# A two-block transformer kernel on one core: the hand-over from the convolution's input product to its output product is re-ordered

## The chip, the cores and the metric

The kernel runs on one core of one Trainium2 chip. The time is the device time of one execution in microseconds (us). The core has TensorE (PE: matmuls; its weight loads are listed as PEld), VectorE (DVE), ScalarE (ACT), GpSimd (POOL) and SyncE (SP, which issues the loads).

## The reference, cut to what matters

Batch 1, 256 tokens, width 2048, float32. The first block is the one that the change touches:

```python
cond = silu(c)
sh1, sc1, g1, sh2, sc2, g2 = split(cond @ mod_w + mod_b, 6)       # "modulation", mod_w is 2048 x 12288
h = rms_norm(x, norm1_g) * (1 + sc1) + sh1
a, gt = split(h @ conv_w_in + conv_b_in, 2)                       # conv-in, 2048 x 4096
u = a * sigmoid(gt)                                               # the gated units
u = depthwise_causal_conv(u, conv_dw_w, 31 taps) + conv_dw_b
u = silu(layer_norm(u, conv_ln_g, conv_ln_b))                     # over the 2048 channels
x = x + (1 + g1) * (u @ conv_w_out + conv_b_out)                  # conv-out, 2048 x 2048
h = rms_norm(x, norm2_g) * (1 + sc2) + sh2
x = x + (1 + g2) * (relu(h @ mlp_w1)**2 @ mlp_w2)
```

A second block (attention, gated feed-forward, final norm) follows. It is not touched.

## The kernel before

**One stream of loads.** All weights come in one ordered list, `stream`, in tiles of 512 KB, issued by SP in that order. A load goes into a slot and waits until the tile that was in the slot has been read. Up to `n_first` items there are 12 slots; behind it there are 6 (`slot_of`, `earlier_in_slot`), because slots 6 to 11 (`stage2`) lie in the same memory as `whi` and `wlo`, the split copies of conv-out's weights. `consume()` handles the next item of the stream: it emits the instructions that read it. Kinds: "n" is a conv-in tile (multiplied in plain float32), "w" a tile that ACT rounds into `whi` and DVE (or POOL) subtracts into `wlo` for three-pass matmuls (ring of three, `NPAIR`), "m" a tile of modulation weights.

**Modulation.** A group of 16 "m" tiles gives 1024 modulation columns. There are three ways to sum it: on DVE (a multiply, then 15 multiply-adds in a buffer of `accs`), "aside" (ACT multiplies, POOL adds; three product buffers), or on PE (`mod_on_pe`: two one-row matmuls a tile, accumulated in two banks). `mod_end` turns the sum into columns by 8 small matmuls and `mod_columns` (three small DVE instructions). Block 0 has 80 aside tiles (`mods`): 66 (`N_MOD_IN`) go with conv-in, 4 (`N_MOD_TAIL`) into the tail, 10 in among conv-out's tiles 3 to 13. The fourth quarter of norm 2 is summed on PE, all 16 tiles in the tail.

**Emission.** The program is one Python pass; each engine executes its own queue strictly in the order of emission. While products are emitted, `between_tiles()` runs after each PE tile: up to two `tasks`, up to two `delayed` tasks whose tile has come (`later(n, task)`), one of `slow`, up to `TAPS_A_TILE` steps of `dve_taps`, one of `pe_taps`. `run_one()` takes the first of `tasks`, or if none is left the first of `delayed`, due or not.

**The convolution.** Conv-in is 8 chunks p = 0..7 of 8 tiles; chunk p gives the gated units `U` of channel tiles 2p and 2p+1. Its epilogue: ACT evacuates two banks; one tile later `gated` emits 8 transposes (PE), two sigmoids (ACT) and two DVE instructions that write `U`. The taps of 14 channel tiles run on DVE (`DVE_JOBS`; a step is two 128x256 multiply-adds; job (11, 12) and job (13,) become ready with chunk 6, job (15,) with chunk 7), those of tiles 3 and 14 on PE (`pe_job`, 31 matmuls with diagonal matrices, in parts of 8). When channel tiles 0 to 12 are done, `ln_provisional` sums them on PE and DVE makes the provisional mean `m0`; 7 `centre` steps subtract it (DVE), their squares go through ACT and PE (`ln_square`). Tiles 13, 14, 15 follow in `ln_late`. Then `layer_norm()` and its `finish` tasks make `hhi`/`hlo`, conv-out's left side.

**The tail** is the code in `build_program` behind `products(0, n1)`: the rest of the tasks, then a loop with two tasks, one part of `pe_taps`, up to four steps of taps, one of `slow` and one `consume()` a turn. Then all tail tiles are consumed, and, ahead of `layer_norm()`,

```python
while len(pair_ready) < 2:
    consume()
```

which puts the splits of conv-out's first two weight tiles in front of the layer norm in every queue.

## Time and profile before

| | |
|---|---|
| time, median of 3 runs | 2690.1 us (2689.15 to 2693.38) |
| the profiled execution's own time | 2690.38 us |
| its span in the trace | 2688.1 us |
| TensorE busy | 2541.3 us (95%) |
| VectorE, ScalarE, GpSimd busy | 1755.5, 1146.5, 373.6 us |
| conv-in's last part, tail, conv-out (windows) | 141.6 to 332.7, to 424.6, to 531.5 us |
| HBM read | 640.60 MB |

The span runs from the first to the last instruction. A busy share is an average over all stages; the tail is where TensorE's share falls most in this part. In the timeline each row is a run of like instructions of one engine: start, length, what it does, how many, and in brackets how long the engine had been idle and what ended that.

### The profile page before, as it was taken

The page shows a single profiled execution, that of the slowest core. Times are in us where ns is not written, and L with a number is a line of the kernel's source. Part 1 is how long each engine was busy: PE and PEld are TensorE (multiplying, and loading weights), DVE is VectorE, ACT ScalarE, POOL GpSimd, SP SyncE. Part 2 cuts the span into 40 slices and gives each one's busy share as a digit, 9 for nine tenths or more (in the row PEclk, how much of TensorE's full clock was granted, in tenths as well). Part 3 has the DMA queues.
Part 4 walks back from the last instruction along what each step waited for, and adds up shares of the span by engine and source line. Part 5 has one row for each costly group of instructions (what it writes and reads, how often), then busy time and mean ns, then how long its engine had stood idle before and what let it go on. Part 6 is the DMA issues. An engine that isn't in the chain of part 4 may idle for free.

```text
span 2688.1 us, 29379 instructions
## 1 busy us (share of the span) xinstructions
PE 2541.3 (95%) x10784; PEld 1977.6 (74%) x10784; DVE 1755.5 (65%) x2124; ACT 1146.5 (43%) x1441; POOL 373.6 (14%) x177
## 2 busy tenths in 40 slices
PE   4899977989999999999899999999899999999998
PEld 2354444778888888888678788788688888888886
DVE  5678847677877867768665455786577654555455
ACT  2144426444344344344445454544444434443443
POOL 1048823112222222222000000000000000000000
PEclk9999988989999999999899999999899999999999
DMA  8989736668888888888754647886488766666664
GB/s 299 375 294 386 250 120 220 209 210 297 301 301 283 308 289 302 305 293 291 195 169 129 180 134 222 304 273 225 157 282 275 241 189 194 188 189 194 190 188 141
DMA packets 340158, 644.66 MB, mean 240 GB/s; under 512 B 30000, under 2 KB 63440, under 8 KB 338992
## 3 DMA queue, kind: packets, MB, share of 16 engines
q1 hardware_dynamic: 338752, 642.09, 73.1%
q8 instruction: 87, 1.43, 0.2%
q0 software_dynamic: 448, 0.43, 0.1%
q14 instruction: 55, 0.45, 0.1%
q10 hardware_dynamic: 816, 0.26, 0.0%
HBM read 640.60 MB, written 2.10 MB: 239 GB/s over the span
## 4 chain that ended last, share of the span: by engine, by line
PE 83%; DVE 8%; DMA 4%; ACT 2%; POOL 2%; issue 1%; SPq 0%; DVEq 0%; ACTq 0%; POOLq 0%
PE bank L84 83%; DVE bank L84 3%; DMA stage<-in_mod_w 2%; DVE wlo L84 1%; POOL R L84 1%; DVE acc L84 1%; DVE scr L84 1%; ACT whi L84 1%; ACT scr L84 1%; DVE X L84 1%; DVE R2f L84 0%; DVE R L84 0%; DMA stage<-in_w_in 0%; SPq L84 0%; DMA stage<-in_mlp_w 0%
## 5 line engine op out<-in xcount | busy, mean ns | idle before, releaser
L84 DVE TENSOR_TENSOR wlo<-stage,whi 128x1024 fp32r<-128x1024 f32 x688 | 868.4, 1264 | 673.7 <-ACT whi L84 653.8
L84 ACT ACTIVATE whi<-stage 128x1024 fp32r<-128x1024 f32 x752 | 795.8, 1059 | 1022.3 <-PE bank L84 921.7
L84 PE MATMUL bank<-whi,hhi 128*128 128x512 f32 x2016 | 806.5, 400 | 31.6 <-DVE hlo L84 18.9
L84 PE MATMUL bank<-wlo,hhi 128*128 128x512 f32 x2016 | 791.6, 393 | 0.0
L84 PE MATMUL bank<-whi,hlo 128*128 128x512 f32 x2016 | 791.3, 393 | 0.0
L84 PEld LDWEIGHTS bank<-whi,hhi 128*128 128x128 f32 x2016 | 383.2, 190 | 119.2 <-ACT scr L84 23.5
L84 PEld LDWEIGHTS bank<-wlo,hhi 128*128 128x128 f32 x2016 | 383.3, 190 | 81.0 <-issue 3.1
L84 PEld LDWEIGHTS bank<-whi,hlo 128*128 128x128 f32 x2016 | 382.7, 190 | 81.4
L84 PE MATMUL bank<-whi,uhi 128*128 128x512 f32 x992 | 390.0, 393 | 0.8 <-POOL wlo L84 0.8
L84 PE MATMUL bank<-whi,ulo 128*128 128x512 f32 x992 | 389.8, 393 | 0.0
L84 PE MATMUL bank<-wlo,uhi 128*128 128x512 f32 x992 | 387.0, 390 | 0.0
L84 POOL TENSOR_TENSOR wlo<-stage,whi 128x1024 fp32r<-128x1024 f32 x64 | 166.0, 2594 | 632.1 <-ACT whi L84 620.7
L84 PE MATMUL bank<-stage,hx 128*128 128x512 f32 x512 | 234.0, 615 | 10.1 <-DMA stage<-in_conv_w_in 5.8
L84 DVE SCALAR_TENSOR_TENSOR acc<-stage,CS,acc 128x1024 f32<-128x1024 f32 x165 | 213.1, 1292 | 17.1 <-DMA stage<-in_mod_w 15.0
L84 POOL TENSOR_TENSOR R<-R 128x1024 f32<-128x1024 f32 x75 | 183.1, 2443 | 270.6 <-ACT R L84 262.8
L84 PEld LDWEIGHTS bank<-wlo,uhi 128*128 128x128 f32 x992 | 186.3, 188 | 41.8 <-issue 0.2
L84 PEld LDWEIGHTS bank<-whi,uhi 128*128 128x128 f32 x992 | 186.4, 188 | 40.9 <-issue 2.2
L84 PEld LDWEIGHTS bank<-whi,ulo 128*128 128x128 f32 x992 | 186.3, 188 | 40.7
L84 PEld LDWEIGHTS bank<-stage,hx 128*128 128x128 f32 x512 | 99.4, 197 | 134.8 <-issue 120.9
L84 DVE SCALAR_TENSOR_TENSOR bank<-R2f,DW,bank 128x256 f32<-128x256 f32 x418 | 165.4, 483 | 0.0
L84 DVE SCALAR_TENSOR_TENSOR R<-stage,CS,R 128x1024 f32<-128x1024 f32 x105 | 134.3, 1279 | 13.9 <-DMA stage<-in_mod_w 11.6
L84 PE MATMUL bank<-ident,scr 128*128 128x128 f32 x524 | 81.3, 299 | 38.2 <-DVE scr L84 33.3
(120 smaller groups left out, 1182.9 us busy)
## 6 DMA issues: line engine op xcount, KB each, us to landing
stage<-in_mlp_w SPq DMA_DIRECT2D x256, 512.0 KB, 5.4
stage<-in_mod_w SPq DMA_DIRECT2D x192, 512.0 KB, 7.6
stage<-in_w_ada SPq DMA_DIRECT2D x192, 512.0 KB, 5.2
stage<-in_w_in SPq DMA_DIRECT2D x136, 512.0 KB, 3.9
stage<-in_w_ffn_gate SPq DMA_DIRECT2D x88, 512.0 KB, 4.4
stage<-in_w_ffn_up SPq DMA_DIRECT2D x88, 512.0 KB, 4.4
stage<-in_w_ffn_down SPq DMA_DIRECT2D x88, 512.0 KB, 4.2
stage<-in_conv_w_in SPq DMA_DIRECT2D x128, 256.0 KB, 7.7
```

The lines of the kernel that those rows point to most:

```text
L84: made = fn(*args, **kw)
```

## The change

It has five parts.

1. **Slots.** `n_first` grows by the length of the tail, so the tail's tiles use all 12 slots. The two conv-out tiles ahead of `layer_norm()` are no longer consumed there.
2. **Modulation.** The tail holds 8 tiles of the last group (PE) and 9 aside tiles, 17 in place of 20. The group's other 8 tiles go on in a buffer of `accs` on DVE (`mod_goes_on`: one multiply, two adds of the PE row onto one row of the buffer, 7 multiply-adds), among conv-out's tiles 3 to 18 with the 5 aside tiles that are left. Its columns come by the ordinary `mod_end`.
3. **Pace of the taps.** In place of 5 steps a tile, steps are emitted until an estimate of their end passes the estimate of the tile's end by `LEAD` (8, from the ninth tile before the end of conv-in 2); in the tail three steps a turn in place of four.
4. **Gated units.** The epilogue is cut into `turn` (transposes, sigmoids) and `gated` (the DVE part and what follows), emitted 2 and 3 tiles later; for p < 3 one tile later, and for the last chunk at once. `L_SQUARE` is 3.
5. **Tail.** After the tasks, four tiles are consumed at once. Tile 14's 31 tap matmuls are one part; its evacuation (`pe_ends`) is emitted only when no DVE taps are left. The warming square root is left out of conv-in, and a Silu is emitted behind the layer norm's square root.

```diff
-N_MOD_TAIL = 4
-N_MOD_OUT = 14
-TAPS_A_TILE = 5
+N_MOD_TAIL = 9
+N_MOD_PE = 8
+N_MOD_OUT = 18
+LEAD = 8.0
+LEAD_LAST = 2.0
+TILE_US = 4.1
+STEP_US = 0.8
...
-L_SQUARE = 2
+L_SQUARE = 3
+L_TURN = 2
+L_GATED = 3
...
+        pace = {"tile": 0.0, "taps": 0.0, "lead": LEAD}
...
             for _ in range(min(len(slow), 1 + len(slow) // 10)):
...
-            for _ in range(min(len(dve_taps), TAPS_A_TILE)):
+            pace["tile"] += TILE_US
+            if not dve_taps:
+                pace["taps"] = max(pace["taps"], pace["tile"])
+            while dve_taps and pace["taps"] < pace["tile"] + pace["lead"]:
+                pace["taps"] += STEP_US
...
-                if m["aside"] == "PE":
+                if m["aside"] == "PE" and kt < N_MOD_PE:
...
+                elif m["aside"] == "PE":
+                    mod_goes_on(m, kt, w, c, landed)
+                    stage_free[s] = [m["last"]]
                 elif m["aside"]:
...
-                                  start=(kt == 0), stop=(kt == NKT - 1), signal=(j == 1),
+                                  start=(kt == 0), stop=(kt == N_MOD_PE - 1), signal=(j == 1),
...
+        def mod_goes_on(m, kt, w, c, landed):
+            if kt > N_MOD_PE:
+                m["last"] = V.put(nc.vector.scalar_tensor_tensor, out=m["buf"][1], in0=w, scalar=c,
+                                  in1=m["buf"][1], op0=ALU.mult, op1=ALU.add, after=[landed, m["last"]])
+                return
+            run_until(accs.any_free)
+            m["buf"] = accs.take()
+            m["ring"] = accs
+            rows, buf = m["last"], m["buf"][1]
+            t = V.put(nc.vector.tensor_scalar, buf, w, c, None, ALU.mult, after=[landed, m["cond"]] + m["buf"][2])
+            for j in range(2):
+                row = buf[0:1, j * 512:(j + 1) * 512]
+                m["last"] = V.put(nc.vector.tensor_tensor, row, row, groups[m["group"]][j][0:1, :], ALU.add,
+                                  after=[t, rows])
+            group_free[m["group"]] = [m["last"]]
         def mod_columns(m, bank, t):
...
         def mod_end(m):
...
-            if m["aside"] == "PE":
-                row = []
-                for j in range(2):
-                    row.append(tiles.take())
-                    i, buf, free = row[j]
-                    row[j] = (i, buf, A.put(nc.scalar.activation, buf[0:1, :], groups[m["group"]][j][0:1, :], ACT.Copy,
-                                            after=[m["last"]] + free))
-                group_free[m["group"]] = [row[0][2], row[1][2]]
-                def columns():
-                    b, bank, free = misc.take()
-                    for j in range(8):
-                        _, buf, made = row[j // 4]
-                        t = T.put(nc.tensor.matmul, bank[:, j:j + 1], buf[0:1, (j % 4) * 128:(j % 4) * 128 + 128],
-                                  ones[0:1, 0:1], start=True, stop=True, after=[made, consts] + free)
-                    for i, _, _ in row:
-                        tiles.give(i, t)
-                    misc.give(b, mod_columns(m, bank, t))
-                later(2, columns)
-                return
...
+        pe_ends = deque()
...
-                if hi_ == TAPS:
+                def end():
...
-            for lo in range(0, TAPS, 8):
-                pe_taps.append(lambda lo=lo: part(lo, min(lo + 8, TAPS)))
+                if hi_ == TAPS:
+                    if ct == PE_JOBS[0]:
+                        end()
+                    else:
+                        pe_ends.append(end)
+            for lo in range(0, TAPS, 8 if ct == PE_JOBS[0] else TAPS):
+                pe_taps.append(lambda lo=lo: part(lo, min(lo + (8 if ct == PE_JOBS[0] else TAPS), TAPS)))
...
-                    def gated():
-                        two = [misc.take(), misc.take()]
+                    state = {}
+                    def turn():
+                        two = state["two"] = [misc.take(), misc.take()]
...
-                        i, sig, free = tiles.take()
+                        state["values"] = t
+                        state["sig"] = i, sig, free = tiles.take()
...
-                            r = A.put(nc.scalar.activation, sig[:, k * S:(k + 1) * S], two[1][1][:, k * S:(k + 1) * S],
-                                      ACT.Sigmoid, bias=PA[:, 32 + ct:33 + ct], after=[gates_in, params["A"]] + free)
+                            state["sigmoid"] = A.put(nc.scalar.activation, sig[:, k * S:(k + 1) * S],
+                                                     two[1][1][:, k * S:(k + 1) * S], ACT.Sigmoid,
+                                                     bias=PA[:, 32 + ct:33 + ct],
+                                                     after=[gates_in, params["A"]] + free)
+                        misc.give(two[1][0], state["sigmoid"])
+                    def gated():
+                        b, bank, _ = state["two"][0]
+                        i, sig, _ = state["sig"]
...
-                                                in0=two[0][1][:, k * S:(k + 1) * S], scalar=PA[:, 16 + ct:17 + ct],
+                                                in0=bank[:, k * S:(k + 1) * S], scalar=PA[:, 16 + ct:17 + ct],
...
-                                                after=[t, r, params["A"], consts])
-                        misc.give(two[1][0], r)
-                        misc.give(two[0][0], u_ready[ct])
+                                                after=[state["values"], state["sigmoid"], params["A"], consts])
+                        pace["taps"] += STEP_US
+                        misc.give(b, u_ready[ct])
...
-                    later(1, gated)
+                    if p == NKT // 2 - 1:
+                        tasks.append(turn)
+                        tasks.append(gated)
+                    elif p < 3:
+                        later(1, turn)
+                        later(1, gated)
+                    else:
+                        later(L_TURN, turn)
+                        later(L_GATED, gated)
...
+                    pace["taps"] += STEP_US
...
+            A.put(nc.scalar.activation, ST[:, 62:63], eps, ACT.Silu, after=[consts])
...
-        tail = mix(mod_pairs(0, 1, 3, aside="PE", soon=True), mods[N_MOD_IN:N_MOD_IN + N_MOD_TAIL])
-        seq += tail + co[:3] + mix(co[3:N_MOD_OUT], mods[N_MOD_IN + N_MOD_TAIL:]) + co[N_MOD_OUT:]
-        n_tail = n_first[0] + len(tail)
+        last = mod_pairs(0, 1, 3, aside="PE")
+        tail = mix(last[:N_MOD_PE], mods[N_MOD_IN:N_MOD_IN + N_MOD_TAIL])
+        seq += tail + co[:3] + mix(co[3:N_MOD_OUT], mods[N_MOD_IN + N_MOD_TAIL:] + last[N_MOD_PE:]) + co[N_MOD_OUT:]
+        n_tail = n_first[0] = n_first[0] + len(tail)
...
-                if g == hi_ - 6:
+                if g == n1 - 9:
+                    pace["lead"] = LEAD_LAST
+                if g == hi_ - 6 and lo:
...
-        while tasks or delayed:
+        while tasks:
...
-            for _ in range(min(len(dve_taps), 4)):
+        for _ in range(4):
+            consume()
+        while dve_taps or pe_taps or slow or tasks or delayed or pe_ends or len(ln["late"]) < len(LN_LATE):
+            if pe_taps:
+                pe_taps.popleft()()
+            for _ in range(min(len(dve_taps), 3)):
...
-        while dve_taps or pe_taps or slow or tasks or delayed or len(ln["late"]) < len(LN_LATE):
+            if not dve_taps and pe_ends:
+                pe_ends.popleft()()
...
-            if pe_taps:
-                pe_taps.popleft()()
-            for _ in range(min(len(dve_taps), 4)):
-                dve_taps.popleft()()
...
-            consume()
-        while len(pair_ready) < 2:
...
```

## Rows read from the trace of the kernel before

**Rows 1.** The page: its span.
```profile
span 2688.1 us, 29379 instructions
```

**Rows 2.** Windows: PE, PEld, DVE, ACT, POOL busy (count), granted clock, DMA share, GB/s.
```profile
141.60:332.70 191.10, 186.95 (x510) 92.16 (x511) 154.47 (x389) 90.51 (x120) 143.98 (x67) 0.98 0.90 313
332.70:424.60 91.90, 66.56 (x215) 35.42 (x214) 46.79 (x99) 29.88 (x43) 24.18 (x11) 0.84 0.49 162
424.60:531.50 106.90, 98.84 (x416) 79.63 (x416) 76.23 (x69) 59.06 (x75) 29.77 (x10) 0.93 0.64 199
```

**Rows 3.** Timeline of PE: conv-in's end, the tail, conv-out's beginning.
```profile
274.26 0.33 PE L84 MATMUL bank<-ident,scr 128*128 128x128 f32 x1 [3.06 <-ACT scr L84]
...
275.89 22.12 PE L84 MATMUL bank<-stage,hx 128*128 128x512 f32 x48
...
308.67 24.20 PE L84 MATMUL bank<-stage,hx 128*128 128x512 f32 x56
332.71 5.78 PE L84 MATMUL bank<-R2f,ones 128*128 128x256 f32 x26
345.94 3.58 PE L84 MATMUL bank<-ones,R 128*128 128x1 f32 x16 [7.45 <-POOL R L84]
...
392.06 20.76 PE L84 MATMUL bank<-stage,CS 128*1 128x512 f32 x48
...
424.61 0.76 PE L84 MATMUL bank<-whi,hhi 128*128 128x512 f32 x1 [11.79 <-DVE hlo L84]
...
432.22 1.94 PE L84 MATMUL bank<-ones,scr 1*128 1x1 f32 x16
```

**Rows 4.** Timeline of DVE, chunk 6's gated units to conv-out.
```profile
309.67 0.88 DVE L84 SCALAR_TENSOR_TENSOR R2f<-bank,PA,scr 128x256 f32<-128x256 f32 x2 [5.61 <-ACT scr L84]
...
311.36 23.59 DVE L84 SCALAR_TENSOR_TENSOR bank<-R2f,DW,bank 128x256 f32<-128x256 f32 x60
...
338.98 2.21 DVE L84 TENSOR_TENSOR R2f<-R2f,scr 128x512 f32<-128x512 f32 x1
...
353.03 0.87 DVE L84 SCALAR_TENSOR_TENSOR R2f<-bank,PA,scr 128x256 f32<-128x256 f32 x2
...
380.60 0.42 DVE L84 TENSOR_TENSOR R2f<-R2f,scr 128x256 f32<-128x256 f32 x1 [8.07 <-ACT R2f L84]
380.94 0.48 DVE L84 SCALAR_TENSOR_TENSOR bank<-R2f,DW,bank 128x256 f32<-128x256 f32 x1
...
414.38 2.59 DVE L84 TENSOR_TENSOR wlo<-stage,whi 128x1024 fp32r<-128x1024 f32 x2 [30.09 <-ACT whi L84]
...
494.84 1.23 DVE L84 TENSOR_TENSOR wlo<-stage,whi 128x1024 fp32r<-128x1024 f32 x1 [1.49 <-ACT whi L84]
```

**Rows 5.** Timeline of ACT, same stretch.
```profile
304.10 0.66 ACT L84 ACTIVATE R2f<-bank 128x256 f32<-128x256 f32 x2 [10.95 <-DVE bank L84]
...
338.25 1.15 ACT L84 ACTIVATE R<-stage,CS 128x1024 f32<-128x1024 f32 x1 [0.81 <-POOL R L84]
339.30 1.06 ACT L84 ACTIVATE scr<-bank 128x512 f32<-128x512 f32 x2
...
351.25 0.84 ACT L84 ACTIVATE scr<-bank,PA 128x256 f32<-128x256 f32 x2 [9.59 <-PE bank L84]
...
418.26 0.51 ACT L84 ACTIVATE scr<-scr,ST 128x256 f32<-128x256 f32 x1 [1.10 <-DVE scr L84]
```

**Rows 6.** Groups by form in the tail, PE: tile 14's taps.
```profile
L84 PE MATMUL bank<-R2f,hx 128*128 128x256 f32 x62 | 16.1, 417 | 0.0
```

**Rows 7.** Groups by form in conv-out, DVE: count, busy us, mean ns, idle before.
```profile
L84 DVE TENSOR_TENSOR wlo<-stage,whi 128x1024 fp32r<-128x1024 f32 x30 | 53.3, 1799 | 24.3 <-ACT whi L84 22.1 <-issue 2.3
L84 DVE TENSOR_TENSOR scr<-bank,G 128x512 f32<-128x512 f32 x6 | 4.1, 684 | 0.0
```

**Rows 8.** The tile `acc` from 250 to 650 us: duration ns min/median/max.
```profile
L84 DVE SCALAR_TENSOR_TENSOR acc<-stage,CS,acc x15: 1273/1279/3422, 562.1 to 622.8; 128x1024 f32<-128x1024 f32 x15
L84 DVE TENSOR_SCALAR acc<-stage,CS x1: 734/734/734, 535.5 to 535.5; 128x1024 f32<-128x1024 f32 x1
```

## The prediction

> **What bounds the kernel now.** First the windows [rows 2]: up to 332.7 us PE is busy 186.95 of 191.10 us, in the tail 66.56 of 91.90, in conv-out 98.84 of 106.90. DMA moves 162 GB/s in the tail against 313 before it, so the change is about the tail and what it takes from its neighbours. The timelines then say what the tail waits for. PE's last wait ends with DVE's `hlo` [rows 3]. DVE does its last tap at 380.94, its last small work near 384, and then stands 30.09 us until conv-out's first `whi` exists [rows 4]: the two splits stand ahead of the layer norm in its queue, their weights stand behind the modulation tiles in the stream, and PE reads the last twelve of these in 20.76 us, 1.73 each [rows 3]. So the end of the tail is set by stream order, not by the convolution. Before that, DVE waits 8.07 us for tile 14's evacuation with one step of taps unfinished [rows 4]; and chunk 7's units, whose transposes stand behind columns that wait 7.45 us for POOL, reach DVE at 353.03 although conv-in ends at 332.5 [rows 3, 4]. With the stream out of the way, DVE's work and its own waits set the end.
>
> **The change step by step. (a) When chunk 7's units come.** Chunk 6's went to DVE at 309.67 [rows 4]. Their transposes move one PE tile back, 24.20/7 = 3.46 us [rows 3]; against that PE's stall of 3.06 us at 274.26, a wait for an evacuation that ACT could not start, gets a tile of slack and goes, with some 1.5 us of half-rate matmuls behind it (behind it 6 tiles took 22.12 us where 6 x 3.46 = 20.7 were due [rows 3]). That leaves 309 (up to 313 if the stall's time isn't kept). Job (11, 12) takes 309.67 to 334.95, 25.3 us [rows 4], so it ends at 334.3; ACT evacuates it (0.66, as [rows 5], first) and does the sigmoid (0.84 [rows 5]), and DVE the first unit (0.44 [rows 4]): tile 14's `U` is there at 336.3. The other path is POOL: the last conv-in product on ACT stood at 338.25, and the evacuation right behind it [rows 5]. If POOL keeps its time, evacuation, transposes (1.0), sigmoid and unit give 343; part of its backlog came from ACT standing 10.95 us for a tap evacuation [rows 5], and should shrink. I take 338, bounds 335.5 and 343.
>
> **(b) A new stall on DVE.** Counting steps through `between_tiles` with the new pace (4.1 a tile, 0.8 a step, lead 2 from tile 55), 7 steps go out after tile 58, then 5, 5, 5, 6, and 5 after tile 63: the 32nd of job (11, 12), its end, is among the last, with one step of job 13. So `ln_provisional` is still in `delayed` when the tail begins. The loop's first turn emits, in this order: all 31 tap matmuls of tile 14 (PE), three steps of job 13 (DVE, 2.4 us), the columns of the aside group (PE, then three small DVE instructions), the sums of tiles 0 to 12 (PE), `m0` (DVE). PE's queue is in order: taps 16.1 us [rows 6], columns 3.58, sums 5.78 [rows 3], `m0` 0.43. `m0` ends at 338 + 0.4 + 16.1 + 3.6 + 5.8 + 0.4 = 364.3, and DVE, which reaches it near 341.5, has stood over 20 us. Before, the sums ran right behind conv-in and the taps came in four parts with squares between. This is what the part of 31 costs; its gain is that nothing of it waits later. Everything behind on DVE (taps, centring) waits with it; ACT's squares too. The columns' wait for POOL (345.94 before [rows 3]) hides under the taps.
>
> **(c) From `m0` to the layer norm's root.** DVE has left 23 taps of tile 13 and 31 of tile 15, at 23.59/60 = 0.393 and a little more for first ones: 21.7 us. Seven centrings lie between 0.68 alone (the same size in [rows 7]) and 2.21 beside POOL [rows 4]; nine aside tiles now run there, not four, so I take 7.3 in all (bounds 4.6 and 15). Tile 13's end and centring: 1.3. Last tap at 394.6. Tile 14's evacuation no longer stops a tap (8.07 us saved, but it now follows): copy, add, centring, square of 15, then the same of 14, about 4.9 us to the end of the root, from the spacing of those steps before. Root at 399.5.
>
> **(d) To the first matmul of conv-out.** Before, from the root's end (418.77 [rows 5]) to 424.61: 5.84, with one split in it. Now three splits (1.22 each, of which two come extra, the slots holding the weights already) stand before the first `finish`: 5.84 + 2.44 = 8.3. Start at 407.8, against 424.61: **16.8 us gained**. Loads can't take it back: twelve slots let the 17 tiles and conv-out's first ones be issued turns ahead, and SP waited for consumption.
>
> **(e) Tail tiles.** PE sheds 8 x 1.73 = 13.8 us, but in (b) it isn't this that DVE waits for, so I book nothing. If it were needed behind `m0`, PE has 8 squares and 7 tiles, some 21 us, under DVE's 30.
>
> **(f) Conv-out, 106.90 us before.** The columns of the last group are now 16 full-height records, 3.58 in place of 1.94 [rows 3]: +1.6. The bank pair of the half group is now freed by DVE's two row adds at k = 8, which conv-out's second chunk needs: DVE does split, multiply (0.734 [rows 8]) and two adds, each under 0.684 (full height, same width [rows 7]), after a split that itself waits for PE: +2 (bounds 0 and 6). DVE gets 0.73 + 7 x 1.28 + 1.3 = 11.0 us of new work [rows 7, 8]. Against it, splits cost 1.799 us on average [rows 7] where undisturbed ones cost 1.23 [rows 4], 17 us of 53.3, and five of ten aside tiles leave conv-out: about 8.5 back. Conv-out's later tiles come every 1.23 + 1.49 = 2.72 us and leave DVE idle for the 1.49 [rows 4], which holds a 1.28 multiply-add. Three more loads stand in the mixed stretch. For these together +0.5 (bounds -5 and +16). Sum **+4.1**.
>
> **(g)** The table loads left out of conv-in (ACT) and the Silu load lie beside other work: nothing, at most 1.3 us each.
>
> **Sum.** The profiled execution took 2690.38, its span 2688.1 [rows 1]; 2690.4 - 16.8 + 4.1 = 2677.7. The runs' median is 0.3 lower: **2677.5**.
>
> **Rivals.** *No stall at `m0`*: if the sums get ahead of tile 14's taps (my count of steps is one off only at the last tile, and one more turn would not do it, but an early `run_one` would), DVE runs through from 338.9: `m0` 0.4, 60 taps 24.1, centring and tile 13's end 8.3, root at 376.6, first matmul at 384.9, 23 us sooner: 2654.6. For it speaks that 30.09 and 8.07 us of waits are there to be had [rows 4]; against it the order of emission. Chance 0.14.
>
> *DVE becomes conv-out's bound* (the other side): new work 11.0 us not hidden at all, and half contended. [Rows 8] show a multiply-add of 3.42 us beside one of POOL's subtractions, 2.14 over the median; 7 x 2.14/2 = 7.5. With +1.6 and +2, conv-out is 22.1 longer, and the time is 2690.4 - 16.8 + 22.1 = 2695.7, 2695.4 at the median. It decides once more than 16.8 us of conv-out's additions show. Against it: POOL's adds end before most of these multiply-adds are due. Chance 0.10. The Trainium skill, GPSIMD Engine Reference, section Specifications, says that GpSimd's SBUF interfaces are shared with VectorE and contend when a VectorE instruction has two SBUF inputs, which this multiply-add has and the taps (PSUM accumulator) have not; it speaks against moving tiles to DVE while POOL adds. The trace agrees where both run [rows 7, 8]; by the rule with every one of the seven contended the time would be 7.5 us more again, 2702.9.
>
> *PE's tail stays at half rate.* The tap matmuls of tile 14 started at the lower of TensorE's two clocks after PE had idled; the granted clock of the tail is 0.84 [rows 2]. A 512-wide record at the upper clock takes 20.76/48 = 0.43 us [rows 3], so a 256-wide one at the lower takes as much; 62 of them are 26.8 in place of 16.1 us: `m0` 10.7 later, 2688.2. Chance 0.08; all 62 took 16.1 before.
>
> **How the numbers follow.** My forecast has 0.60, the rivals 0.14, 0.10, 0.08, and 0.08 is for what I haven't seen. The likeliest case's own range: (a) -2.5 to +5, (c) -3 to +8, (f) -7 to +8, not all at one end: 2668 to 2688. To hold 8 in 10 it reaches down to the no-stall case and up to the clock case: **2655 to 2689**. A measurement tells about 0.2% (5.4 us) from no change. Faster by more (below 2684.7): most of the forecast, 0.52, the first rival 0.14, and 0.07 of the rest: 0.73. Within: 0.14. Slower: 0.13.
>
> **What the profile would show.** (a) DVE writes chunk 7's units at 336 to 343, with ACT's tap evacuation just before the sigmoid. (b) PE shows 62 records of `R2f,hx` in one row, then the columns, then 26 of `R2f,ones`; DVE stands about 17 us before `MC` and again before the small `scr<-bank`, 20 to 24 in all. If these waits are missing, the first rival holds. (c) Last tap near 395, no 8 us wait in front of it. (d) The 30.09 us wait is gone, and three `wlo` stand between the reciprocal and the first `hlo`. (f) conv-out lasts 107 to 115 us; a wait of PE for DVE's `acc` or `R` at the second chunk; splits near 1.23 us once POOL is quiet. Wrong I would be through a wait on a load in the tail, through POOL's nine aside tiles holding ACT (which every square and evacuation passes), or through conv-out running longer than 123 us.

## The result and the profile after

The changed kernel takes 2695.7 us (median of 20 runs) against 2689.8 of the kernel before in the same rounds (20 runs): ratio 1.0021, 95% interval 1.0014 to 1.0028. It is slower by 6 us. The prediction said 2677.5, faster, with a range of 2655 to 2689. The profiled execution took 2699.4, its span is 2697.1. Of all runs in this document one, of *units early*, fell in a slower state of the chip (3212 us at a granted clock of 0.76) and is not counted. In what follows L90 is the same recording helper as L84 before.

The windows of the kernel after, over the same three stretches as [rows 2]:

```profile
141.60:332.70 191.10, 181.27 (x489) 90.14 (x489) 142.20 (x357) 83.81 (x113) 133.38 (x63) 0.97 0.86 301
332.70:424.60 91.90, 64.40 (x204) 34.36 (x203) 62.55 (x129) 36.56 (x49) 46.53 (x20) 0.85 0.48 160
424.60:531.50 106.90, 90.39 (x379) 73.59 (x380) 74.29 (x77) 51.62 (x68) 14.53 (x5) 0.89 0.63 205
```

All three stretches hold less of PE's work than before. The first is a surprise: it lies ahead of the tail, I had costed nothing in it, and it lost 5.7 us of PE and 12.3 of DVE. PE's timeline after, with the time that it stood and the releaser at the end of a row:

```profile
172.51 1.94 PE L90 MATMUL bank<-ident,scr 128*128 128x128 f32 x8 [3.51 <-DVE R2f L90]
...
251.05 0.33 PE L90 MATMUL bank<-ident,scr 128*128 128x128 f32 x1 [1.65 <-ACT scr L90]
...
284.16 0.33 PE L90 MATMUL bank<-ident,scr 128*128 128x128 f32 x1 [2.11 <-ACT scr L90]
...
318.51 0.33 PE L90 MATMUL bank<-ident,scr 128*128 128x128 f32 x1 [2.00 <-ACT scr L90]
...
339.57 2.74 PE L90 MATMUL bank<-stage,hx 128*128 128x512 f32 x6
351.08 2.24 PE L90 MATMUL bank<-ident,scr 128*128 128x128 f32 x8 [8.77 <-ACT scr L90]
...
356.56 13.65 PE L90 MATMUL bank<-R2f,hx 128*128 128x256 f32 x62
370.05 1.84 PE L90 MATMUL bank<-ones,R 128*128 128x1 f32 x16
371.76 5.86 PE L90 MATMUL bank<-R2f,ones 128*128 128x256 f32 x26
...
412.68 4.39 PE L90 MATMUL bank<-stage,CS 128*1 128x512 f32 x8
425.39 0.76 PE L90 MATMUL bank<-whi,hhi 128*128 128x512 f32 x1 [8.32 <-ACT scr L90]
...
466.98 0.77 PE L90 MATMUL bank<-whi,hhi 128*128 128x512 f32 x1 [8.29 <-DVE acc L90]
```

Where [rows 3] had one wait of 3.06 us on its way to the tail (and the same timeline one of 0.77), there are four now, 9.3 us in all, with half-rate matmuls behind them (eight transposes in 1.94 us at 172.51, in 1.04 at 169.16 before), and conv-in's last products end at 342.3 in place of 332.7 or so. Chunk 7's transposes then wait 8.77 us more for ACT. The 62 tap records, the columns and the sums come in the order that step (b) said. Conv-out's first matmul starts at 425.39, which is 0.8 *later* than before, and in conv-out there is a new wait of 8.29 for the row adds. DVE's timeline after:

```profile
156.61 14.98 DVE L90 SCALAR_TENSOR_TENSOR bank<-R2f,DW,bank 128x256 f32<-128x256 f32 x38
171.49 0.88 DVE L90 SCALAR_TENSOR_TENSOR R2f<-bank,PA,scr 128x256 f32<-128x256 f32 x2
...
321.85 0.88 DVE L90 SCALAR_TENSOR_TENSOR R2f<-bank,PA,scr 128x256 f32<-128x256 f32 x2 [6.64 <-ACT scr L90]
...
353.45 0.88 DVE L90 SCALAR_TENSOR_TENSOR R2f<-bank,PA,scr 128x256 f32<-128x256 f32 x2 [5.49 <-ACT scr L90]
354.24 2.44 DVE L90 SCALAR_TENSOR_TENSOR bank<-R2f,DW,bank 128x256 f32<-128x256 f32 x6
371.93 0.23 DVE L90 TENSOR_TENSOR MC<-bank,PB 128x4 f32<-128x4 f32 x2 [15.25 <-PE bank L90]
...
377.65 0.43 DVE L90 TENSOR_SCALAR scr<-bank 128x256 f32<-128x256 f32 x1 [5.29 <-PE bank L90]
...
449.47 12.74 DVE L90 TENSOR_TENSOR wlo<-stage,whi 128x1024 fp32r<-128x1024 f32 x4 [0.56 <-issue]
462.13 0.68 DVE L90 TENSOR_TENSOR scr<-bank,G 128x512 f32<-128x512 f32 x1
...
464.77 0.75 DVE L90 TENSOR_SCALAR acc<-stage,CS 128x1024 f32<-128x1024 f32 x1
465.56 1.27 DVE L90 TENSOR_TENSOR acc<-acc,bank 1x512 f32<-1x512 f32 x2
```

The 30.09 us wait of [rows 4] is gone. In its place DVE stands 15.25 + 5.29 us at the start of the tail, and everything starts later. The first two rows show where the conv-in part goes wrong. In the kernel before 18 taps stand between the units of chunks 0 and 1, and PE's transposes find the bank free:

```profile
156.93 7.14 DVE L84 SCALAR_TENSOR_TENSOR bank<-R2f,DW,bank 128x256 f32<-128x256 f32 x18
163.98 0.87 DVE L84 SCALAR_TENSOR_TENSOR R2f<-bank,PA,scr 128x256 f32<-128x256 f32 x2
```

Now 38 do, because the pace lets the taps run 8 us ahead: fifteen steps go out at once. The other end of it is on ACT, whose tap evacuations stand in its queue until DVE's last tap, with POOL's products behind them. ACT after:

```profile
247.78 0.66 ACT L90 ACTIVATE R2f<-bank 128x256 f32<-128x256 f32 x2 [13.16 <-DVE bank L90]
...
281.93 0.66 ACT L90 ACTIVATE R2f<-bank 128x256 f32<-128x256 f32 x2 [11.43 <-DVE bank L90]
...
315.24 0.66 ACT L90 ACTIVATE R2f<-bank 128x256 f32<-128x256 f32 x2 [12.33 <-DVE bank L90]
...
349.40 1.15 ACT L90 ACTIVATE R<-stage,CS 128x1024 f32<-128x1024 f32 x1 [1.34 <-POOL R L90]
```

Of these the first was 3.85 before, the second 11.32, the third 10.95 [rows 5]. ACT's last product of conv-in comes at 349.40 where it came at 338.25 [rows 5], and chunk 7's evacuation stands right behind it.

### The profile page after: what moved, and what is told of

It reads as the page before. It is cut to its first block, busy times and chain, and to the rows that moved or that the text cites. A ratio compares the mean times of both kernels' runs of the same rounds, so it can differ in the third digit from the quotient of the medians.

```text
span 2697.1 us, 29330 instructions
## 1 busy us (share of the span) xinstructions
PE 2534.3 (94%) x10752; PEld 1976.7 (73%) x10752; DVE 1763.1 (65%) x2134; ACT 1142.9 (42%) x1437; POOL 369.7 (14%) x177
## 4 chain that ended last, share of the span: by engine, by line
PE 83%; DVE 8%; POOL 3%; DMA 3%; ACT 2%; issue 1%; SPq 0%; DVEq 0%; ACTq 0%; POOLq 0%
PE bank L90 83%; DVE bank L90 3%; POOL R L90 3%; DMA stage<-in_mod_w 2%; DVE wlo L90 1%; DVE scr L90 1%; DVE R2f L90 1%; ACT scr L90 1%; ACT whi L90 1%; DVE acc L90 1%; DVE X L90 0%; ACT hhi L90 0%; DMA stage<-in_w_in 0%; DMA stage<-in_conv_w_out 0%; ACT R L90 0%
## 5 line engine op out<-in xcount | busy, mean ns | idle before, releaser
L90 DVE TENSOR_TENSOR wlo<-stage,whi 128x1024 fp32r<-128x1024 f32 x688 | 859.8, 1251 | 648.4 <-ACT whi L90 634.5
L90 ACT ACTIVATE whi<-stage 128x1024 fp32r<-128x1024 f32 x752 | 795.5, 1059 | 1036.8 <-PE bank L90 928.0
L90 PE MATMUL bank<-whi,hhi 128*128 128x512 f32 x2016 | 806.1, 400 | 39.3 <-ACT scr L90 8.3
L90 PE MATMUL bank<-whi,hlo 128*128 128x512 f32 x2016 | 791.3, 393 | 0.0
L90 PE MATMUL bank<-wlo,hhi 128*128 128x512 f32 x2016 | 791.1, 392 | 0.0
L90 PEld LDWEIGHTS bank<-whi,hhi 128*128 128x128 f32 x2016 | 382.9, 190 | 126.2 <-ACT scr L90 17.1
L90 PEld LDWEIGHTS bank<-wlo,hhi 128*128 128x128 f32 x2016 | 383.1, 190 | 80.9 <-issue 3.1
L90 PEld LDWEIGHTS bank<-whi,hlo 128*128 128x128 f32 x2016 | 382.3, 190 | 81.5
L90 PE MATMUL bank<-whi,ulo 128*128 128x512 f32 x992 | 389.7, 393 | 0.0
L90 PE MATMUL bank<-whi,uhi 128*128 128x512 f32 x992 | 389.7, 393 | 0.0
L90 PE MATMUL bank<-wlo,uhi 128*128 128x512 f32 x992 | 387.1, 390 | 0.0
L90 POOL TENSOR_TENSOR wlo<-stage,whi 128x1024 fp32r<-128x1024 f32 x64 | 165.5, 2585 | 658.0 <-ACT whi L90 650.7
L90 PE MATMUL bank<-stage,hx 128*128 128x512 f32 x512 | 235.0, 617 | 7.4 <-DVE hx L90 4.2
L90 DVE SCALAR_TENSOR_TENSOR acc<-stage,CS,acc 128x1024 f32<-128x1024 f32 x172 | 220.0, 1279 | 15.6 <-DMA stage<-in_mod_w 13.5
L90 PEld LDWEIGHTS bank<-wlo,uhi 128*128 128x128 f32 x992 | 186.3, 188 | 41.8 <-issue 0.2
L90 PEld LDWEIGHTS bank<-whi,ulo 128*128 128x128 f32 x992 | 186.3, 188 | 40.6
L90 PEld LDWEIGHTS bank<-whi,uhi 128*128 128x128 f32 x992 | 186.4, 188 | 39.6 <-issue 0.5
L90 POOL TENSOR_TENSOR R<-R 128x1024 f32<-128x1024 f32 x75 | 179.6, 2397 | 255.7 <-ACT R L90 247.7
L90 PEld LDWEIGHTS bank<-stage,hx 128*128 128x128 f32 x512 | 100.3, 199 | 131.5 <-issue 121.8
L90 DVE SCALAR_TENSOR_TENSOR bank<-R2f,DW,bank 128x256 f32<-128x256 f32 x418 | 165.2, 482 | 0.0
L90 DVE SCALAR_TENSOR_TENSOR R<-stage,CS,R 128x1024 f32<-128x1024 f32 x105 | 136.4, 1299 | 12.7 <-DMA stage<-in_mod_w 10.2
L90 PE MATMUL bank<-ident,scr 128*128 128x128 f32 x524 | 83.0, 301 | 52.2 <-DVE scr L90 33.3
```

The lines of the kernel that those rows point to most:

```text
L90: made = fn(*args, **kw)
```

## The experiments

Each was timed in five rounds beside the kernel before, whose medians lay between 2688.5 and 2690.8. Differences between two rows below are differences of their medians, and good to about 2 us for that reason. "Conv-out starts" is the first matmul with `whi`.

| run | us | ratio to before, 95% interval | conv-out starts |
|---|---|---|---|
| changed kernel | 2695.7 | 1.0014 to 1.0028 | 425.4 |
| units early | 2691.3 | 0.9993 to 1.0012 | 421.2 |
| fixed pace | 2681.4 | 0.9959 to 0.9981 | 411.6 |
| lead 2 | 2679.5 | 0.9951 to 0.9975 | 408.5 |
| pace and units | 2676.5 | 0.9935 to 0.9965 | 407.5 |
| row first | 2688.4 | 0.9984 to 1.0005 | 424.2 |
| parts of 8 | 2685.0 | 0.9975 to 0.9996 | 415.7 |
| pace, units, row | 2668.3 | 0.9910 to 0.9937 | 406.1 |
| all four edits | 2658.2 | 0.9871 to 0.9896 | 395.3 |
| all four, six slots | 2661.5 | 0.9884 to 0.9911 | 398.8 |
| all four, 12 tiles on PE | 2654.0 | 0.9857 to 0.9882 | 397.3 |
| all four, 15 on PE | 2662.3 | 0.9880 to 0.9907 | 406.3 |
| the same, six slots | 2668.3 | 0.9897 to 0.9928 | 412.4 |
| before, no splits ahead of the norm | 2688.2 | 0.9986 to 1.0003 | 424.7 |
| the same, twelve slots | 2686.9 | 0.9980 to 0.9998 | 421.8 |

**Units early.**

```
-L_TURN = 2
-L_GATED = 3
+L_TURN = 1
+L_GATED = 1
```

> The changed kernel with the transposes, sigmoids and gated units emitted one tile behind their chunk, as before the change. Theory A (units that come late hold ScalarE in front of tap evacuations, and so GpSimd's sums and TensorE's transposes): GpSimd's last sum before the tail's ends some 4 to 8 us earlier than its 361.6 us, and since the tap job of tiles 11 and 12 is then emitted before conv-in ends, the provisional sums stand ahead of tile 14's taps and VectorE's stall of 15 + 5 us before m0 shrinks to a few us; time about 2680 us. Theory B (GpSimd's own rate of 2.5 us an add sets chunk 7's units, whatever the order): GpSimd's last sum stays within 2 us of 361.6, chunk 7's units at 353; only the stall changes, time 2685 to 2690.

2691.3. Theory A gave 2680 and is wrong for this edit by itself; theory B's 2685 to 2690 doesn't hold either. The waits for tap evacuations stay (13.47, 15.41 and 13.63 us on ACT), PE stands 3.50 us at 170.75 as in the changed kernel, and chunk 7's units come at 359.45, 6.0 *later* than there. What is gained lies behind them: `m0` now stands ahead of tile 14's taps (DVE starts it at 349.62, for 377.65), though 15.62 us of wait in front of `MC` stay.

**Fixed pace.**

```
-            while dve_taps and pace["taps"] < pace["tile"] + pace["lead"]:
-                pace["taps"] += STEP_US
+            for _ in range(min(len(dve_taps), 5)):
                 dve_taps.popleft()()
```

> The changed kernel with five steps of taps a tile again, in place of the paced emission; units stay late. Theory A: the wait of TensorE for VectorE at 172 us (3.5 us) goes, since 15 steps no longer stand ahead of chunk 1's units; the waits of ScalarE for a tap evacuation (13.2, 11.4, 12.3 us) shrink by one to two tiles' time each where they are not fed by the loop; conv-in ends 4 to 8 us earlier; the stall before m0 stays; time about 2689 us. Theory B: conv-in's last units at 353, time 2694 to 2697.

2681.4, 14.3 us less than the changed kernel, and well below the 2689 of theory A. ACT's longest wait for a tap evacuation is 8.37 us, as in the kernel before; PE stands only 1.37 us in conv-in and 5.23 in front of chunk 7's transposes, and chunk 7's units come at 335.70; the stall on DVE stays (13.42 in front of `MC`). That the pace costs is shown; whether through its lead or its clock the run on the lead tells.

**Pace and units.** The two edits above together.

> Both: units one tile behind their chunk and five steps of taps a tile, so conv-in is emitted as before the change, with the change's tail, slots and modulation behind it. Theory A: conv-in as before (last product near 332.5, GpSimd's last sum near 346), chunk 7's units near 343 since nothing stands before them, no stall of 20 us before m0, first conv-out matmul near 400; with conv-out's added 7.6 us the time is about 2674 us. Theory B: the tail's end moves by the stall alone, first matmul 405 to 410, time 2680 to 2685. If the tail's own parts were the loss, the time stays near 2695.

2676.5, conv-out at 407.5: between what the two theories gave. Chunk 6's units come as before the change (309.70), chunk 7's 8.0 us sooner than there (345.03), and `m0` gets ahead of tile 14's taps (DVE does it at 339.99), which is the "no stall" rival's condition. Yet 13.07 us of wait in front of `MC` stay, since the columns are still emitted behind the 31 taps. So the rival was half right: there are two things behind the taps, and either holds DVE.

**Row first.** The half group's ninth tile, whose row adds free the bank pair, moves ahead of the other modulation tiles.

```
-... mix(co[3:N_MOD_OUT], mods[N_MOD_IN + N_MOD_TAIL:] + last[N_MOD_PE:]) ...
+... mix(co[3:N_MOD_OUT], last[N_MOD_PE:N_MOD_PE + 1] + mods[N_MOD_IN + N_MOD_TAIL:]
+                         + last[N_MOD_PE + 1:]) ...
```

> The changed kernel with the ninth tile of the half-and-half modulation group (the one whose row adds free the pair of banks) first among the tiles mixed into conv-out, in place of sixth. Theory: TensorE's wait of 8.3 us for VectorE's row adds at 467 us, and some 2 us at the lower clock behind it, go; VectorE has the same work earlier, where it is the bound, so 1 to 3 us come back; time 2687 to 2690. Rival: the splits of conv-out's weights, held up by GpSimd and by loads, would have made TensorE wait there anyway; the wait then changes its releaser and the time stays within 2 us of 2695.7.

2688.4, 7.3 us less, with conv-in and tail as in the changed kernel. PE's timeline in conv-out has no wait for `acc` left:

```profile
446.45 0.76 PE L90 MATMUL bank<-whi,hhi 128*128 128x512 f32 x1 [5.88 <-DVE wlo L90]
...
465.70 0.47 PE L90 MATMUL bank<-whi,hhi 128*128 128x512 f32 x1 [2.27 <-DVE wlo L90]
```

**Parts of 8.** Tile 14's taps in four parts, as before.

```
-            for lo in range(0, TAPS, 8 if ct == PE_JOBS[0] else TAPS):
+            for lo in range(0, TAPS, 8):
```

> The changed kernel with tile 14's 31 taps given out in four parts (8, 8, 8, 7) as before the change; nothing else. Theory A (the stall on DVE is one of order in PE's queue: the columns and the sums stand behind 62 records of taps): the wait in front of MC falls from 15.25 to about 4 us, m0 comes some 10 us sooner (368 in place of 378), and conv-out's first matmul near 415 in place of 425.4; the conv-in part stays as in the changed kernel. Time 2684 to 2688. Theory B (what sets the end of the tail is something else, the load stream, POOL or ACT's evacuations, and DVE's standing lies beside it): the wait shrinks but conv-out begins at 423 to 425 all the same; 2693 to 2697.

2685.0, 10.7 us less, by this edit alone. Theory A's time and its `m0` (367.93) hold, and the wait in front of `MC` is 5.45. DVE:

```profile
362.21 0.23 DVE L90 TENSOR_TENSOR MC<-bank,PB 128x4 f32<-128x4 f32 x2 [5.45 <-PE bank L90]
...
367.93 0.43 DVE L90 TENSOR_SCALAR scr<-bank 128x256 f32<-128x256 f32 x1 [5.29 <-PE bank L90]
```

**Lead 2.**

```
-LEAD = 8.0
+LEAD = 2.0
```

> The changed kernel with one number edited: the taps are given out at most 2 us ahead of the tiles' clock from the start, in place of 8; so nearly as five a tile, with the units still late. Theory A (what costs in conv-in is the lead: the taps given out ahead stand in DVE's queue before the next chunk's units, and one chunk's 30 us of taps come in a burst before it): ACT's waits for tap evacuations fall from 11 to 13 us to under 9, PE's waits for them go but for one, conv-out begins near 411; 2680 to 2685. Theory B (the lead does nothing; counting by a clock of 4.1 us a tile, with the two extra entries for the units, is what falls out of step with the tiles): 2692 to 2697.

2679.5, 16.2 us less than the changed kernel by one number: theory A, just below its bounds. Counting by a pace costs nothing that shows (the fixed pace gave 2681.4); the lead does. PE's waits in conv-in, then chunk 7's units and `m0` on DVE:

```profile
275.11 1.09 PE L90 MATMUL bank<-ident,scr 128*128 128x128 f32 x8 [0.39 <-ACT R2f L90]
...
294.80 1.98 PE L90 MATMUL bank<-R,ones 128*128 128x512 f32 x4 [1.42 <-POOL R L90]
...
333.79 2.24 PE L90 MATMUL bank<-ident,scr 128*128 128x128 f32 x8 [5.23 <-ACT scr L90]
```

```profile
336.15 0.88 DVE L90 SCALAR_TENSOR_TENSOR R2f<-bank,PA,scr 128x256 f32<-128x256 f32 x2 [0.69 <-ACT scr L90]
...
360.75 0.42 DVE L90 TENSOR_SCALAR scr<-bank 128x256 f32<-128x256 f32 x1 [5.30 <-PE bank L90]
```

**Pace, units and row together.**

> The changed kernel with three edits: five steps of taps a tile in place of the paced bursts, the gated units one tile after their chunk as before, and the half group's ninth tile first among conv-out's modulation tiles. Theory A (the costs are separate and add): the pace and the units gave 2676.5 together, the row 7.3 alone; so 2669 (2667 to 2672), with PE's wait for acc (7.68 us there) gone. Theory B (with conv-out beginning 17 us earlier its splits collide with POOL's sums, so the row adds are late whatever their order): 2674 to 2677.

2668.3, 8.2 less than without the row. The costs are separate.

**All four.** Beside these, parts of 8, and the tail's loop takes them up behind the delayed tasks:

```
+            for _ in range(2):
+                if tasks or delayed:
+                    run_one()
             if pe_taps:
                 pe_taps.popleft()()
             ...
-            for _ in range(2):
-                if tasks or delayed:
-                    run_one()
```

> As the run before it (pace, units, row), and tile 14's taps in parts of 8 that stand behind the delayed tasks in the tail's loop, so that the columns of the aside group come ahead of them. Theory A (what is left of the stall, 13.07 us in front of MC with pace and units mended, lies on the path to conv-out): 8 to 12 us less than the run before, 2657 to 2661, conv-out's first matmul at 396 to 399. Theory B (the stall is cover for POOL's sums, for tile 14's evacuation or for conv-out's weights, one of which is late next): 0 to 4 us less, 2665 to 2669, with a new wait of 8 us or more in front of the last taps, the centring or the first whi.

2658.2, 10.1 less again, in theory A's range. DVE waits 2.41 us in front of `MC`, and PE has the columns first:

```profile
342.72 2.23 PE L90 MATMUL bank<-ones,R 128*128 128x1 f32 x16 [2.84 <-POOL R L90]
...
346.65 5.77 PE L90 MATMUL bank<-R2f,hx 128*128 128x256 f32 x16
...
379.02 5.31 PE L90 MATMUL bank<-stage,CS 128*1 128x512 f32 x12
395.26 0.76 PE L90 MATMUL bank<-whi,hhi 128*128 128x512 f32 x1 [10.92 <-ACT scr L90]
```

The next four runs ask which part of the change takes away the 30.09 us wait of before.

**Before, without splits ahead of the norm.**

```
-        while len(pair_ready) < 2:
-            consume()
```

> The kernel before with one part of the change alone: the loop that splits two tiles of conv-out ahead of the layer norm is left out, so that the norm's small work no longer stands behind the splits in DVE's and ACT's queues. Theory A, my prediction's reading of the 30.09 us wait (the splits are in the norm's way, and the norm was ready long before): the norm ends some 25 us sooner, conv-out begins as soon as its first weights have come, at 416 to 418 in place of 424.6; 2682 to 2684. Theory B (the weights of conv-out land late, and the three splits and the first finish then cost as much behind the norm as ahead of it): conv-out begins within 2 us of 424.6; 2688 to 2691.

2688.2 with an interval that holds 1, conv-out at 424.65: theory B. DVE now stands 22.03 us for ACT's square root, which stands in ACT's queue behind products that wait for their tiles (9.57, 8.79 and 5.58 us for loads). The splits were not what held the norm.

**The same with twelve slots.**

```
-        n_tail = n_first[0] + len(tail)
+        n_tail = n_first[0] = n_first[0] + len(tail)
```

> The kernel before with two parts of the change alone: twelve slots through the tail, and no splits ahead of the layer norm; order of taps, pace, units and the half group as before. Theory A (these two take the stream out of the tail's end, and the rest of the change is what gives it back): DVE's 22 to 30 us of waiting at the norm goes, the norm's root ends near 392, conv-out begins at 400 to 408 in place of 424.6; 2666 to 2675. Theory B (the sixteen tiles on TensorE still come too late for it, being read in order at 1.73 us each behind tile 14's taps): conv-out begins at 415 or later, 2680 to 2689.

2686.9, conv-out at 421.82: theory B. The root now ends at 406.3, yet little is won by it. PE reads the last twelve tiles just as before, and the first `whi` starts as it ends. PE, then ACT:

```profile
393.13 20.76 PE L84 MATMUL bank<-stage,CS 128*1 128x512 f32 x48
421.82 0.77 PE L84 MATMUL bank<-whi,hhi 128*128 128x512 f32 x1 [7.92 <-DVE hlo L84]
```

```profile
403.19 1.15 ACT L84 ACTIVATE R<-stage,CS 128x1024 f32<-128x1024 f32 x1 [8.73 <-DMA stage<-in_mod_w]
...
413.98 2.95 ACT L84 ACTIVATE whi<-stage 128x1024 fp32r<-128x1024 f32 x3 [7.72 <-issue]
```

The profile names no releaser for the 7.72 us, but the code does: the buffers of `whi` share memory with the second six slots, so the first `whi` has to wait until PE has read the last modulation tile in them (413.89).

**All four, six slots.** The line above undone.

> The run with all four edits (pace, units, row, parts behind the columns; 2658.2), but the twelve load slots end with conv-in, as before the change: six through the tail and conv-out. Theory A (the tail's end was set by the stream before the change, and the slots are what takes it away; this was what my prediction's gain rested on): the loads are late again, ACT and PE wait for modulation tiles, conv-out begins at 408 to 418 in place of 395.3, 2672 to 2680. Theory B (the order written in the tail is enough, and the loads come in time from six slots too): conv-out begins within 3 us of 395.3, 2657 to 2661.

2661.5: 3.3 us more than with twelve, conv-out 3.6 us later, just outside theory B's bounds. With eight tiles on PE the slots are worth about 3 us; the two intervals overlap a little.

**All four, twelve tiles on PE.** `N_MOD_PE = 12` in place of 8.

> The run with all four edits, with twelve of the half group's sixteen tiles on TensorE in the tail in place of eight, so four multiply-adds fewer on DVE in conv-out and four loads more in the tail. Theory A (with twelve slots the tail has room for them, as my step that booked nothing for PE's share says, and conv-out's start is set by DVE's taps): conv-out begins within 3 us of 395.3, its mixed stretch is 3 to 6 us shorter, 2653 to 2657. Theory B (the stream is the next limit of the tail: a tile of 0.5 MB takes 1.7 us at the 301 GB/s of conv-in): conv-out begins 7 us later and 3 to 6 come back, 2659 to 2663.

2654.0, the fastest version, 34 us under the 2688.5 of the kernel before beside it. Conv-out starts 2.0 later and the rest is shorter by more: theory A.

**All four, fifteen tiles on PE**, and **the same with six slots**.

> The run with all four edits, but fifteen of the half group's sixteen tiles on TensorE in the tail (one left for DVE): the twelve slots with the modulation of before. Theory A (PE's own reading of the tiles, 1.73 us each behind the squares, sets the tail's end, as the 48 records of 20.76 us that end at 413.9 in the run with slots alone say): from twelve to fifteen tiles conv-out begins 5 to 10 us later than the 397.3 of twelve tiles, 2658 to 2664. Theory B (PE has room under DVE's taps, and it was the order of emission alone that held the tail): conv-out begins within 3 us of 397.3; 2651 to 2656.

> As the run before it, with six load slots in the tail. Theory A (slots and PE's share act on one limit: with all the tiles in the tail the stream is late again, and the slots are worth much more than the 3.3 us that they were worth with eight): 8 us or more over the run before it, 2666 or more, with ACT or PE waiting for modulation tiles. Theory B (the slots are worth the same 2 to 4 us here): 2 to 4 us over it.

2662.3, and conv-out starts at 406.3, 9.0 later than with twelve tiles: theory A of the first. PE reads its tiles until 395.0; only then does SP issue conv-out's first load (395.01, after 11.7 us without one), and `whi` waits 6.11 us for it. With six slots it is 2668.3, 6.0 us more: between what the two theories gave, with the waits for modulation tiles that theory A named (four on ACT, 1.57 to 3.90 us, and one of 1.78 on PE). So the slots are worth somewhat more when more tiles pass, but not 8 us. PE and ACT with fifteen and twelve slots:

```profile
381.09 13.89 PE L90 MATMUL bank<-stage,CS 128*1 128x512 f32 x32
406.30 0.77 PE L90 MATMUL bank<-whi,hhi 128*128 128x512 f32 x1 [11.32 <-ACT scr L90]
```

```profile
399.14 1.06 ACT L90 ACTIVATE whi<-stage 128x1024 fp32r<-128x1024 f32 x1 [6.11 <-DMA stage<-in_conv_w_out]
```

## Why the prediction was wrong

Against the 2677.7 of the sum the profiled execution took 2699.4, 21.7 more. Conv-out started 17.6 late (425.4 for 407.8) and took 3.4 more (PE ends it near 539.8: 114.4 for 106.9 + 4.1); the remaining 0.7 lies behind it.

**(a) When chunk 7's units come: the step that failed.** I took 338 with bounds 335.5 and 343; they came at 353.45, 15.4 late, most of the whole error. I worked from 309.67 for chunk 6's, "up to 313", which took conv-in's rhythm as untouched, and counted the new pace only at its end, for the order in (b). But the lead acts from the first chunk: chunk 6's units came at 321.85. The same rule that put fifteen steps at once into DVE's queue was in the diff, and the two prices stood in the rows: 0.393 us a tap, so 20 taps more before chunk 1's units are 7.9 us; and an ACT evacuation that stands 10.95 us [rows 5], with POOL's products behind it. I used the second as a reserve ("should shrink"); it grew, 36.9 us in three waits where it was 26.1, and the last product came 11.2 later. Most of it is there early: chunk 2's units come at 180.89 for 172.59, 8.3 late, chunk 6's 12.2. How it divides between the burst and ACT's waits no run separates. With lead 2 both go (chunk 1's units at 165.59, ACT's three waits 4.86, 2.49 and 4.95), so the lead makes both. Cut to 2 it gives 16.2 us back, the fixed pace 14.3, and chunk 7's units come inside my bounds, at 336.15 and 335.70. With lead 2 the rest follows nearly as summed: `m0` ends at 361.2 for 364.3, conv-out starts at 408.5 for 407.8, the time is 2679.5 for 2677.5. The later units do bring chunk 7's sooner, as I said: 335.70 for 345.03, both with the fixed pace. Yet they cost some 4 to 5 us of the time (2695.7 to 2691.3 alone; 2681.4 to 2676.5 on top of the pace), because with them `m0` stands behind tile 14's taps: that is the stall in (b), and I had not put it down to them.

**(b) The stall.** Right in mechanism, order and size: 15.25 and 5.29 us, 20.5 in all, where I said 20 to 24; 62 records in one row; from the units to `m0`'s end 24.6 us for 26.3. What it costs the kernel: 10.7 us when only the parts are given back, 10.1 on top of the others, with the loop's new order.

**(c) and (d)** held to 2.4 and 1.4 us: from `m0` to the root 37.6 for 35.2, root to matmul 9.7 for 8.3. Two of the centrings beside POOL took 2.40 us, against 0.68 alone.

**(e) PE's tail tiles at nothing: wrong in what it says of before.** In the sum it did no harm, as I had put the whole gain under (d). But the reading that "the end of the tail is set by stream order", cured by slots, is refuted: slots without splits ahead of the norm gain 2.8 us of conv-out's start in the kernel before, and about 3.3 us of the time in the version with all four edits. What holds the tail of the kernel before is PE's reading, in order, behind the last squares, at 1.73 us a tile: with all else mended 15, 12 and 8 tiles on PE start conv-out at 406.3, 397.3 and 395.3. The last step is 2.0 for four tiles, 6.9 us of reading, so at eight the reading sets the start no more. From fifteen to twelve is 8.3 us of the time by the medians (6.7 by the ratios to the kernel before, 0.9894 and 0.9869); below twelve DVE's share in conv-out costs more than the tail gains (2658.2 with eight for 2654.0). In [rows 3] this limit was to be seen: 48 records without a gap end at 412.8, and ACT's first `whi` starts at 413.2.

**(f) Conv-out.** I had +4.1, it was +7.5. The row adds were the mis-sized term: 2, with bounds 0 and 6, for a wait of 8.29 where PE had waited 2.27 for a split before, so 6.0 more. I had the right queue, but took the splits ahead of them as if alone. Four of them took 12.74 us beside POOL's adds (12.78 before, so this is not new, but nothing on PE waited for row adds behind them), and the residual's own work stands between. Moved first, the row gives 7.3 to 8.2 us.

**The rivals.** *No stall* didn't happen in the changed kernel. With all four edits it nearly did, at 2658.2, 3.6 from its 2654.6; that they lie so close is in part luck, since conv-out started at 395.3 there, not at 384.9, and the row placed first gained 7 to 8 us in conv-out. *DVE becomes conv-out's bound* gave 2695.4, the right time by the wrong way, which is luck: all seven multiply-adds took between 1278 and 1286 ns, none beside POOL, and conv-out was 7.5 longer, not 22.1. By the Trainium skill (GPSIMD Engine Reference, section Specifications), VectorE instructions with two SBUF inputs contend with GpSimd. The trace bears this out for the splits, 3.2 us for 1.23, but POOL was quiet when the multiply-adds came. *PE at half rate*: the 62 records took 13.65 us, not 26.8.

Among the signs of being wrong I had POOL's tiles holding ACT. In part that is what came: ACT's last products ahead of chunk 7's evacuation wait some 1.35 us each for POOL. But I looked for it in the tail and not ahead of it, and POOL had itself stood 8.04 us for ACT (at 317.01), which stood for DVE's taps.

## What to carry to other kernels

A lead is not free on engines that work in order: whatever is given out early stands ahead of what a neighbour waits for, and an evacuation written early makes its engine stand for it. Cost a new order of emission from the first tile that it touches, on every engine, and only then at the place that the change is about. Where a chain of waits ends in a load, look whether another engine's reading ends at the same moment; and put what frees a shared bank ahead of work that nobody waits for.

## What the runs showed of the hardware

A DVE instruction with two SBUF inputs that met one of POOL's 2.35 us adds ended behind that add by nearly its own time, however small it was. With all four edits, the last step of `MC`, 128x4 elements, took 2.16 us in place of 0.16: it ended at 347.41, and POOL's row of five adds (334.97 with 12.42) at 347.39. A centring of half size, 0.42 alone, took 2.14 and ended 0.28 behind its add; a whole one, 0.68 alone, took 2.40 and ended 0.55 behind. So in all three some 0.14 us of the instruction's own time are missing behind the add, and the rest is there. These adds kept their 2.35 us (not so among conv-out's splits, where four took 12.61 in the changed kernel), and the taps, which add into PSUM, their 0.39 or 0.41 us each beside them. DVE, then POOL, with all four edits:

```profile
345.25 2.16 DVE L90 SCALAR_TENSOR_TENSOR MC<-MC,PA 128x4 f32<-128x4 f32 x1
...
352.63 2.40 DVE L90 TENSOR_TENSOR R2f<-R2f,scr 128x512 f32<-128x512 f32 x1
...
365.70 2.43 DVE L90 SCALAR_TENSOR_TENSOR bank<-R2f,DW,bank 128x256 f32<-128x256 f32 x6
368.05 2.14 DVE L90 TENSOR_TENSOR R2f<-R2f,scr 128x256 f32<-128x256 f32 x1
```

```profile
334.97 12.42 POOL L90 TENSOR_TENSOR R<-R 128x1024 f32<-128x1024 f32 x5
352.14 2.34 POOL L90 TENSOR_TENSOR R<-R 128x1024 f32<-128x1024 f32 x1 [4.75 <-ACT R L90]
...
367.56 2.35 POOL L90 TENSOR_TENSOR R<-R 128x1024 f32<-128x1024 f32 x1 [5.28 <-ACT R L90]
```

So the price of such a meeting goes by what is left of POOL's instruction, and is largest, in proportion, for small ones. That it waits for the end, and isn't slowed evenly, is my reading of these few rows; three more in the changed kernel fit it (two whole centrings, 0.54 and 0.55 behind, and a split, 1.23 alone, 1.07 behind), but no run was made for it alone.
